# Routing of a mixture-of-experts stage: logits from unscaled rows, a plan in whole-array steps, and one order of three engines

## The reference

```python
def hierarchical_moe(h, w_router_group, w_router_expert, w1, w3, w2):   # h = rms_norm(x, norm_ffn)
    xf = h.reshape(T, D)
    p_group = softmax(xf @ w_router_group)                  # 4 groups
    g_idx = argmax(p_group);  g_w = p_group[g_idx]
    local = einsum('td,gde->tge', xf, w_router_expert)[g_idx]   # 8 experts of that group
    top_logit, top_idx = top_k(local, 2)
    gate = softmax(top_logit) * g_w
    flat_e = g_idx * 8 + top_idx                            # 2 experts for each token
    # tokens are sorted by expert, each expert's list padded to whole blocks,
    # slot_tok[block, slot] = token, slot_w = its weight, block_e[block] = expert
    for each block:  y[slot_tok] += (silu(xb @ w1[e]) * (xb @ w3[e])) @ w2[e] * slot_w
```

## Time and profile before

| | |
|---|---|
| median of 3 runs | 1912.3 us (1912.04 to 1912.63) |
| profiled execution, its own time | 1909.93 us |
| its span, first to last instruction | 1908.1 us |
| mean granted TensorE clock | 0.945 |
| PE busy / DVE / ACT / POOL | 90% / 60% / 47% / 44% of the span |
| last dense matmul ahead of routing starts | 1266.68 us |
| first matmul of the first expert | 1326.54 us |
| loop over the experts, 29 turns | 1363 to 1886 us, 17.40 or 17.72 us a turn |

### The profile page before, as it was taken

One profiled execution on the slowest core, in us unless ns is written; L12 is line 12 of the kernel. 1 busy time (PEld: TensorE's weight loads), 2 busy tenths in 40 slices (PEclk: granted clock), 3 DMA queues, 4 the chain that ended last, 5 costly groups with the idle time before them and its releaser, 6 DMA issues.

```text
span 1908.1 us, 22953 instructions
## 1 busy us (share of the span) xinstructions
PE 1723.3 (90%) x7380; PEld 1250.9 (66%) x7380; DVE 1142.3 (60%) x1525; ACT 894.8 (47%) x1196; POOL 845.0 (44%) x443
## 2 busy tenths in 40 slices
PE   2899999989998989989689998884999999999996
PEld 2788888777775877458578467672555665666664
DVE  5676673634133265335663314226899999999996
ACT  3544452522323321122422133331788888888885
POOL 0588884242432333113202032110577666776674
PEclk9899999999999999999769998985999999999998
DMA  8343453221321442322104232131899999999994
GB/s 287 99 133 100 121 172 133 95 88 50 101 81 44 155 166 96 125 94 85 38 0 130 88 133 89 44 132 53 311 368 357 374 375 374 372 386 383 378 375 161
DMA packets 135405, 340.92 MB, mean 179 GB/s; under 512 B 14580, under 2 KB 66044, under 8 KB 110504
## 3 DMA queue, kind: packets, MB, share of 16 engines
q1 hardware_dynamic: 127938, 320.69, 46.5%
q0 software_dynamic: 5200, 8.41, 2.0%
q10 hardware_dynamic: 2198, 10.92, 1.5%
HBM read 329.75 MB, written 18.87 MB: 183 GB/s over the span
## 4 chain that ended last, share of the span: by engine, by line
PE 57%; DVE 12%; POOL 12%; issue 11%; ACT 4%; DMA 2%; DVEq 1%; POOLq 0%; ACTq 0%; SPq 0%
PE ps L690 14%; PE ps L692 13%; PE ps L691 13%; PE ps L662 10%; POOL parts L2254 9%; PE ps L672 3%; POOL out L2276 2%; DVE arena L1508 2%; ACT arena L1379 2%; DVE arena L2149 1%; PE ps L1010 1%; PE ps L895 1%; PE ps L1011 1%; PE ps L868 1%; DMA arena<-in_x 1%
## 5 line engine op out<-in xcount | busy, mean ns | idle before, releaser
L2222 POOL TENSOR_TENSOR parts<-ring,parts 128x1024 fp32r<-128x1024 f32 x150 | 372.8, 2491 | 793.4 <-ACT parts L1057 790.2
L1349 ACT CAST parts<-ring 128x1024 fp32r<-128x1024 f32 x384 | 396.2, 1048 | 95.2 <-PE ps L692 71.0
L690 PE MATMUL ps<-parts,act_parts 128*128 128x512 f32 (+2 forms) x1088 | 428.7, 394 | 10.5 <-POOL parts L2254 4.0
L692 PE MATMUL ps<-parts,act_parts 128*128 128x512 f32 (+2 forms) x1088 | 423.9, 390 | 0.0
L691 PE MATMUL ps<-parts,act_parts 128*128 128x512 f32 (+2 forms) x1088 | 423.0, 389 | 0.0
L2045 DVE TENSOR_TENSOR parts<-ring,parts 128x1024 fp32r<-128x1024 f32 x289 | 396.7, 1423 | 26.8 <-ACT parts L1349 20.8
L1057 ACT CAST parts<-ring 128x1024 fp32r<-128x1024 f32 x150 | 155.5, 1047 | 384.6 <-PE ps L692 295.7
L2254 POOL TENSOR_TENSOR parts<-ring,parts 128x1024 fp32r<-128x1024 f32 x95 | 261.0, 2748 | 147.6 <-ACT parts L1349 146.7
L690 PE MATMUL ps<-act_parts,parts 128*128 128x512 f32 x640 | 253.1, 395 | 10.2 <-DVEq L1635 6.0
L692 PE MATMUL ps<-act_parts,parts 128*128 128x512 f32 x640 | 251.0, 392 | 0.0
L691 PE MATMUL ps<-act_parts,parts 128*128 128x512 f32 x640 | 251.0, 392 | 0.0
(11 more groups left out here) (250 smaller groups left out, 1890.6 us busy)
## 6 DMA issues: line engine op xcount, KB each, us to landing
ring<-in_w SPq DMA_DIRECT2D x192, 1024.0 KB, 7.4
ring<-in_w_in SPq DMA_DIRECT2D x30, 1024.0 KB, 7.3
ring<-in_w_in SPq DMA_DIRECT2D x34, 512.0 KB, 5.3
ring<-in_w_ada SPq DMA_DIRECT2D x12, 1024.0 KB, 14.3
ring<-in_w_ret_out SPq DMA_DIRECT2D x8, 1024.0 KB, 6.2
ring<-in_w_out SPq DMA_DIRECT2D x8, 1024.0 KB, 10.2
ring<-in_w_in SPq DMA_DIRECT2D x16, 256.0 KB, 4.1
gates_dram<-arena ACTq DMA_DIRECT2D x8, 512.0 KB, 5.5
```

Source lines behind the costliest of these rows:

```text
L690: pe.matmul(o, lhs[1], rhs[0], start=start, stop=False)
L692: return pe.matmul(o, lhs[0], rhs[0], start=False, stop=stop)
L1349: act.copy(parts[:, n % 4, 0, :], ring[:, j, n % 4 * 1024:(n % 4 + 1) * 1024]).then_inc(piece_hi, 1)
L2222: pool.tensor_tensor(parts[:, g % 4, 1, :], ring[:, st.place(j), k * 1024:(k + 1) * 1024], parts[:, g % 4, 0, :].bitcast(F32), ALU.subtrac ...
```

## The change

**Logits.** Now PE transposes x itself, as soon as the last tile of x is there, and does not wait for h3. The factor g is applied while the bank is copied: DVE copies the even feature tiles, ACT the odd ones, each with the gain as a scalar for each partition (a new row of the column table, `FFN_COL`, brought in by one more 4 KB transfer at the start). The logits are made feature tile by feature tile, into four banks, two tiles behind the transposes. The row's factor `st_r` is applied by DVE to the finished logits, along with -3e38 for the unused columns 4 to 7 (`no_group`). `h3_tok` is still written, between the copies, since the gathers read it. ACT takes a root after each tile's squares.

**Plan.** Loops of small operations on 8, 32 or 64 columns become operations on [128, 4, 32] or [128, 4, 64] views with broadcast operands. The tokens' table is made in two halves, each of which PE may start on. The gate weights, the row of experts by block and the `low`s of the first expert stand behind `slots_ready`. POOL reads the number of blocks ahead of its wait for the slots. The product for the slots' weights (`slot_w`) moves on PE from before the first expert's transposes to behind its up projections, and DVE copies it between `gate` and `hidden` of that block.

```diff
-    ("h3T", KT, 1), ("route", from_bank(1, 5), 1), ("moe0", (0,), 1), ("moe_first", 4, 1),
+    ("h3T", [4 + t % 4 for t in range(KT)], 1), ("route", 8, 1), ("moe0", (0,), 1), ("moe_first", 4, 1),
@@ PE
-            turn_rows("h3T", h3_tok, 3)
+            pe.wait_ge(x_tile_ready, MT)
             pe.wait_ge(ffn_in, 16 * (2 + GROUPS))
-            o = bank("route", 0)
-            nl = GROUPS + EXPERTS
-            for m in range(MT):
-                for t in range(KT):
-                    pe.wait_ge(h3T_ready, t + 1)
-                    mm = pe.matmul(o[:, m * nl:(m + 1) * nl], h3T[:, t, m * P:(m + 1) * P], wr[:, t, :],
-                                   start=(t == 0), stop=(t == KT - 1))
-            filled("route", 0, mm)
+            def logits(t):
+                pe.wait_ge(h3T_ready if t % 2 else h3T_even, t // 2 + 1)
+                for m in range(MT):
+                    o = ps[:, banks["route"].place(m), :] if t else bank("route", m)
+                    mm = pe.matmul(o[:, 0:LOGITS], h3T[:, t, m * P:(m + 1) * P], wr[:, t, :], start=(t == 0), stop=(t == KT - 1))
+                    if t == KT - 1:
+                        filled("route", m, mm)
+            for t in range(KT):
+                turn("h3T", t, [x[:, m, t * P:(t + 1) * P] for m in range(MT)])
+                if t >= 2:
+                    logits(t - 2)
+            for t in (KT - 2, KT - 1):
+                logits(t)
...
-            pe.wait_ge(block_w_ready, 1)
-            filled("route", 4, product(bank("route", 4)[0:SLOTS, 0:64], [slot_oh[:, q, :] for q in range(2 * MT)],
-                                       [block_w[:, q, :] for q in range(2 * MT)]))
             pe.wait_ge(plan_ready, 2)
...
             up("moe_first", 0)
+            pe.wait_ge(block_w_ready, 1)
+            filled("route", 7, product(bank("route", 7)[0:SLOTS, 0:64], [slot_oh[:, q, :] for q in range(2 * MT)],
+                                       [block_w[:, q, :] for q in range(2 * MT)]))
             turn_hidden("moe_first", 0)
@@ ACT
-            act.activation(st_rms[:, 0:MT], st_ms[:, 0:MT], ACT.Sqrt, bias=eps[:, 0:1], scale=1.0 / D).then_inc(rms_ready, 1)
-            for t in range(KT):
-                take("h3T", t, h3T[:, t, :], done=h3T_ready)
+                act.activation(st_rms[:, m:m + 1], st_ms[:, m:m + 1], ACT.Sqrt, bias=eps[:, 0:1], scale=1.0 / D).then_inc(rms_ready, 1)
+            for t in range(1, KT, 2):
+                own(act.activation(h3T[:, t, :], full("h3T", t), ACT.Copy, scale=cols[:, t, FFN_COL:FFN_COL + 1]))
...
@@ DVE
-            reciprocals(0, MT)
             for m in range(MT):
+                t = 2 * m
+                own(dve.tensor_scalar(h3T[:, t, :], full("h3T", t), cols[:, t, FFN_COL:FFN_COL + 1], None, ALU.mult))
+                own.wait()
+                drained("h3T", t, dve.nop())
+                dve.nop().then_inc(h3T_even, 1)
+                reciprocals(m, m + 1)
                 dve.scalar_tensor_tensor(out=h3_tok[:, m, :], in0=x[:, m, :], scalar=st_r[:, m:m + 1], in1=ffn_row,
                                          op0=ALU.mult, op1=ALU.mult).then_inc(row_ready, 1)
+            for m in range(MT):
+                own(dve.scalar_tensor_tensor(out=lg[:, m, :], in0=full("route", m)[:, 0:LOGITS], scalar=st_r[:, m:m + 1],
+                                             in1=no_group, op0=ALU.mult, op1=ALU.add))
...
-            for c in range(2 * MT):
-                own(dve.tensor_scalar(oh[:, c, :], cst("iota")[:, 0:EXPERTS], eid[:, c:c + 1], None, ALU.is_equal))
+            own(dve.tensor_tensor(oh, rows_of(cst("iota")[:, 0:EXPERTS], 2 * MT), spread(eid, EXPERTS), ALU.is_equal))
...
-            for c in range(2 * MT):
-                own(dve.tensor_scalar(slot_oh[:, c, :], cst("iota")[:, 0:SLOTS], inf_[:, c:c + 1], None, ALU.is_equal))
-                own(dve.tensor_scalar(block_oh[:, c, :], cst("iota"), blkf[:, c:c + 1],
-                                      cst("token_off")[:, c % MT:c % MT + 1], ALU.is_equal, ALU.mult))
-            own.wait()
-            dve.nop().then_inc(slot_oh_ready, 1)
+            for q in range(2):
+                part = slice(q * MT, (q + 1) * MT)
+                own(dve.tensor_tensor(block_is[:, part, :], rows_of(cst("iota"), MT), spread(blkf[:, part], 64), ALU.is_equal))
+                own(dve.tensor_tensor(slot_oh[:, part, :], rows_of(cst("iota")[:, 0:SLOTS], MT), spread(inf_[:, part], SLOTS),
+                                      ALU.is_equal))
+                own.wait(1)
+                own(dve.tensor_tensor(block_oh[:, part, :], block_is[:, part, :], spread(cst("token_off"), 64), ALU.mult))
+                own.wait()
+                dve.nop().then_inc(slot_oh_ready, 1)
...
             gate("moe_first", 0)
+            own(dve.tensor_copy(slot_w[0:SLOTS, :], full("route", 7)[0:SLOTS, 0:64]))
+            own.wait()
+            drained("route", 7, dve.nop())
             hidden("moe_first", 0)
@@ POOL
             pool.wait_ge(h3_stored, 16)
+            pool.wait_ge(plan_ready, 1)
+            steps = pool.snap(pool.value_load(n_steps[0:1, 0:1], min_val=EXPERTS - 1, max_val=MAX_BLOCKS - 1))
             pool.wait_ge(slots_ready, 1)
-            steps = pool.snap(pool.value_load(n_steps[0:1, 0:1], min_val=EXPERTS - 1, max_val=MAX_BLOCKS - 1))
```

More of the change, by code:

```diff
@@ L370, in build @@
         y_low = carve([D])
[L371 removed]
+        block_w = block_oh
         slot_w = carve([64])
@@ new lines, in _ @@
+            own(dve.tensor_tensor(counts_over, spread(o[:, MT * EXPERTS:(MT + 1) * EXPERTS], S // SLOTS - 1),
+                                  rows_of(cst("more_blocks"), EXPERTS), ALU.is_gt))
+            own(dve.tensor_scalar(place_e, ranks, float(SLOTS - 1), None, ALU.is_gt))
+            own.wait()
+            own(dve.tensor_reduce(nblk, counts_over, AX.X, ALU.add))
+            own.wait()
+            own(dve.tensor_tensor_scan(incl, cst("ones")[:, 0:EXPERTS], nblk, float(EXPERTS), ALU.mult, ALU.add))
@@ new lines, in _ @@
+            own.wait()
+            own(dve.tensor_tensor(bstart, incl, nblk, ALU.subtract))
+            own.wait()
+            own(dve.tensor_tensor(bstart, bstart, cst("expert_1"), ALU.subtract))
+            own.wait()
+            own(dve.tensor_tensor(place_e, place_e, rows_of(bstart, MT), ALU.mult))
+            own.wait()
+            own(dve.scalar_tensor_tensor(out=place_e, in0=place_e, scalar=float(SLOTS), in1=ranks, op0=ALU.mult, op1=ALU.add))
+            own.wait()
+            drained("route", 4, dve.nop())
@@ new lines, in _, with low @@
+            own.wait()
+            drained("route", 6, dve.nop())
+            dve.nop().then_inc(slots_ready, 1)
+            own(dve.tensor_copy(plan_row[:, :], full("route", 5)[0:1, 0:P]))
+            own.wait()
+            drained("route", 5, dve.nop())
+            dve.nop().then_inc(plan_ready, 1)
+            def low(n, done):
+                dve.wait_ge(piece_hi, done + 1)
+                dve.tensor_tensor(parts[:, n % 4, 1, :], ring[:, n // 4, n % 4 * 1024:(n % 4 + 1) * 1024],
+                                  parts[:, n % 4, 0, :].bitcast(F32), ALU.subtract).then_inc(piece_split[n], 1)
@@ L2072, in _ @@
-            own.wait()
-            dve.nop().then_inc(plan_col_ready, 1)
-            dve.nop().then_inc(plan_ready, 1)
-            expert = cst("iota")[:, 0:EXPERTS]
-            own(dve.tensor_tensor(bstart, bstart, expert, ALU.subtract))
-            own.wait()
-            own(dve.tensor_scalar(bstart, bstart, 1.0, float(SLOTS), ALU.subtract, ALU.mult))
-            own.wait()
-            for m in range(MT):
-                own(dve.scalar_tensor_tensor(out=place_e[:, m, :], in0=ranks[:, m, :], scalar=float(SLOTS - 1), in1=bstart,
-                                             op0=ALU.is_gt, op1=ALU.mult))
@@ L2084, in _ @@
-            own.wait()
-            for m in range(MT):
-                own(dve.scalar_tensor_tensor(out=ranks[:, m, :], in0=expert, scalar=float(SLOTS), in1=ranks[:, m, :],
-                                             op0=ALU.mult, op1=ALU.add))
-            own.wait()
-            own(dve.tensor_tensor(place_e, place_e, ranks, ALU.add))
-            own.wait()
-            for q in range(2):
-                own(dve.tensor_tensor(e_tmp[:, q * MT:(q + 1) * MT, :], oh[:, q * MT:(q + 1) * MT, :], place_e, ALU.mult))
```

185 lines of the change are left out of this document (88 added, 97 removed).

## The result

The changed kernel takes 1891.7 us, the median of four runs (1887.8 to 1892.9), against 1912.5 for the kernel before (1912.0 to 1915.9). The ratio is 0.9881, 95% interval 0.9861 to 0.9900. The forecast was 1892.2. Two more sets of five runs gave 0.9885 (0.9868 to 0.9901) and 0.9873 (0.9855 to 0.9890). So the total was forecast well. Its terms were not: some were off by more than 2 us, and in opposite directions.

The account below looks back on a forecast made before the run. Bound: one unbroken chain of waits from the last dense matmul to the first expert's, PE mostly waiting. Terms 9.7 + 3.85 + 2.45 + 3.85 + 1.9 - 1.6 = 20.15 took 1912.3 to 1892.2 us; 8-in-10 range 1886.5 to 1898.

Parts of the forecast that it names:

- Logits: Last sum of x to DVE's logits read: earlier PE start, clock partly falling, read at 1281.5; gain 9.7 us, bounds 6.8 and 12.7.
- DVE's four rounds: DVE's PSUM copy, reciprocal, semaphores and scaling, 2.25 us a round, four times; fourth copy ends near 1276.4, pacing PE.
- rival 2: Logits stream stays at full clock, paced by DVE's copy rounds: read at 1278.5, total 1889.2 us; chance 20%.
- the cold case: PE at half clock from 1271 on during transposes and logits: read at 1284.4, total 1895.1 us; chance 25%.
- First half of the plan: Logits read to PE's start on the ranks: DVE's small operations merged, 10.45 us down to 6.6, 3.85 gained.
- Ranks: PE's start on the ranks to DVE's read: three DVE subtractions moved away, 4.21 us down to 1.75, 2.45 gained.
- Second half: Ranks' read to PE's start on the slots: whole-array DVE operations, 10.25 us down to 6.4, 3.85 gained.
- slots to POOL: PE's start on the slots to POOL's column copy: first half of PE's work done early, 3.57 us to 1.65, 1.9 gained.
- Cover: DVE's work moved behind the slots stays hidden by gather, transposes and ACT's copy, by 0.3 us; costed at nothing.
- The slots' weights: Their product, now inside the first expert's block, makes later work wait for PE: 1.6 us lost.
- The loop: Unchanged loop keeps nine long turns of 29 (17.71 against 17.40 us); all short would win 2.8, all long lose 6.2.
- rival 3: Loop, entered at another phase, settles in its long turn: total 1898.4 us; chance 8%.

Follow-up runs that it names:

- the experiment: Changed kernel with PE making all 32 transposes first, then all 64 logits, instead of alternating them: 1887.8 us, ratio 0.9891 to the kernel before.
- the held kernel: Changed kernel with PE's transposes of x waiting until DVE has scaled all rows to h3: 1896.2 us, ratio 0.9920 to the kernel before.

## Why the prediction was right, and where its terms were wrong

**The chain.** Read as one unbroken chain without an overlap, it behaved so. Every stretch that was shortened moved what followed by as much, and the first expert came 21.5 us earlier against the last sum of x (59.43 before, 37.98 after).

**Logits, 9.7 against 12.3.** The earlier start was right; the clock was not. I took the middle between a warm and a cold stream, since the earlier trace rows show narrow logits losing the clock. The missing idea is that the order counts. Logits in one run lost the clock in the earlier trace rows and again in the experiment. Alternating with transposes they kept it, in all profiled executions of that order, and in the held kernel too after it had risen. DVE's four rounds (2.39 each, 2.25 forecast) paced nothing that mattered. The forecast's price of a logits instruction, 0.085 and 0.16 us from the windows' counts, was misread: 0.112 and 0.213 are measured. So PE alone needs 7.2 us for the 64 at full clock, not 5.4, and its stream of 11.4 us set the pace. That rival 2's read, 11.39 us after the last sum of x, came so close to the measured 11.78 is luck: rounds that do not bind happen to last about as long as PE's own work, which does bind. At the measured prices the cold case would have come some 3 us later than forecast, an estimate. The Trainium skill's sentence that transposes don't bring the full clock (TensorE: Matmul & The Clock Gate, Part 4: PE-mode transpose), set against the trace in the prediction, would have given the cold case. No execution of the new order showed that one, and by the held kernel too the trace does not agree: its clock rose at 1280.5, after 12 transposes from 1277.78 and two instructions of logits.

**First half of the plan, 3.85 against 1.52.** The step that failed is "four selections of 32 elements 0.5". It took 2.67. The estimate of the operation was right (0.55 with POOL quiet). What was left out is what the operation would now run beside. An earlier chain carried DVE's plan into POOL's subtraction. Without this loss the gain is 3.65, near the forecast.

**Ranks, 2.45 against 2.69.** Right, and shown by putting the subtractions back (2.33).

**Second half 3.85 against 4.70, slots to POOL 1.9 against 0.77.** Together 5.75 against 5.47. The border between the two was wrong: DVE hands over the first half of the table earlier, and PE then takes longer with its 16 instructions (2.26 against 1.97), since the second half is not ready. Repeated operands cost plain time, as chosen.

**Cover, 0 against 0.5 lost.** DVE was ready at 1305.93 and the split waited for ACT until 1307.07, so the cover held by more than the 0.3 forecast. What was lost instead lies in the gather, 4.80 against 4.35 from POOL's copy to the transposes. The preparation of the indirect transfer takes 1.57 on POOL, beside DVE's three subtractions, where it took 1.12 before. With those put back it takes 1.12 again, and the stretch 4.27. So the subtractions are the cause. That the ports are the reason here too was only argued: with the subtractions put back, a product of DVE's (128x512, 0.69 us) lay beside the preparation and did not lengthen it.

**The slots' weights, 1.6.** Right to 0.04: 1.56 once the clock is taken off.

**The loop, held at 9 long turns.** The argument against rival 3, "short turns, once reached, stay to the end", was wrong, and the trace of before already spoke against it: its 7th and 10th turns are short and long ones follow them. Executions with the loop unedited had 1 to 27 long turns, in any order. The price of a turn was right (17.70 against 17.37). The total was hit because 2.6 of luck in the loop met 2.7 of bad luck ahead of the routing, and 2.6 too little for the logits met 2.3 too much for the plan. Three terms were sound; the hit at 1891.7 is partly cancellation. The range of 1886.5 to 1898 was needed for that, and about as wide as the scatter of single runs.

What stays open: why unchanged code ahead of the routing ends between 1261 and 1270. The kept traces account for most of it. Ahead of that sum PE was idle for 117.3 us in the execution with 1261.19 and for 121.7 in that with 1269.83, 4.4 more. It worked 93.2 and 102.2 us at half clock, which at 0.46 a microsecond is 4.1 more, an estimate. Why the clock falls at other times in another execution, and why PE waits more, no run tests.

## What to carry to other kernels

Before you move work on DVE, write down what POOL does at the new time, and the reverse. If DVE's instruction reads two operands from SBUF and POOL's reads SBUF at all, one of 0.2 us can take the other's whole 2.4. Where the two start at the same moment in a loop, the turn's length is a draw; take the small one out of the race by issuing it before its wait. And judge an edit of 1 to 3 us by distances between rows, each within one execution, since whole times scatter by more than that.

## What the runs showed of the hardware that I had not expected

- One DVE operation of 128x32 with both inputs in SBUF took 2311 ns instead of 195 while POOL subtracted tiles of 128x1024. In the loop it is POOL's copy of 64x1 that takes 1268 ns instead of 177, beside a subtraction of DVE's; where the copy wins, that subtraction loses only some 30 ns (1.25 us against 1.22).
- With PE busy all the time, 64 logits of 40 columns in one run lost the full clock after 4.4 us. The same 64 in groups between transposes kept it for 11.4 us. In the held kernel it rose from 0.50 to 1.00 after 12 transposes, 2.7 us from their start, and stayed up for the rest of the stream.
- The same program needed 3.0, 4.8 and 6.1 us of the first expert's block before the clock rose in three executions. Each microsecond of that is worth 0.46 us.
